# Hybrid retention and HGRN2 block on Trainium2: norm weights as 4 KB loads, spread over partitions by matmuls; four x loads on one landing

## The chip, the cores and the metric

The program runs on the 8 NeuronCores of one Trainium2 chip, the same code on each core with its own data: one prompt stream of 2048 frames and two running streams of 16 frames per core. Nothing is exchanged between cores. A time is device microseconds (us) of one execution, taken on the slowest core. The profile is one profiled execution; its page is that of the slowest core (core 7).

The engines are PE (matmuls), ACT, DVE and POOL (elementwise work) and SP, which here only issues DMAs. POOL also issues the DMAs that convert f32 to bf16 on the way, and those that add to their destination. Each engine runs its own list of instructions in order; semaphores order them between engines.

## The reference: what is computed

For x (frames x 1024), with RMSNorm over the 1024 channels before and after:

```
h = rmsnorm(x) * g_pre                      # g_pre: one vector of 1024
u = h @ W_in                                # 1024 x 4096, eight segments of 512 columns
rq, rk, rv, rg, hq, hf, hi, hg = split(u)
retention (4 heads of 128): rotary q, k; decayed state S_ret; o_r
HGRN2     (4 heads of 128): f = lb + (1 - lb) * sigmoid(hf); gated recurrence; o_h
o = concat(silu(rg) * headnorm(o_r), silu(hg) * headnorm(o_h))
y = x + rmsnorm(o @ W_out) * g_post         # g_post: one vector of 1024
```

The new states of both head groups are outputs too.

## The kernel before

**Tiling.** The prompt's 2048 frames are 4 blocks of 4 tiles of 128 frames. `front(k)` does for a block what needs all four tiles: `stage_A` per tile (load x, square sum on ACT at L670, the inverse root on POOL at L673 and L676, scaling by it and by `gpre` on DVE at L679, transposition into `xT` by PE at L693 with an ACT eviction at L697 for blocks 0 and 1, by DMA at L685 later), then `stage_B_hg` per HGRN2 head: the two projections of segments 5 and 4 (L714), the gate on ACT (L766, L768), forward and backward scans on DVE (`fG` L773, `fR` L785), and products on POOL (`KTh` L781, `QTh` L791). The scans work in two sets of buffers, so the projection of a third head waits for the first head's `fR` and `QTh`. `tile(k, j)` does the rest of a tile: the retention projections (segments 0 and 1, L731) with the rotary products (DVE L806, L810, POOL L819), V and gates (segments 2, 6, 3, 7, L731), `stage_D` (scores L895 into `AT`, outputs L927 and L932, new states L944 into `Sst` by DVE at L949 or L952, head norms) and `stage_E` (transposition of `og` into `ogT`, the output projection L1009, the norm with `gpost` at L1027, the residual). A block of two short sample streams follows with block 3; its states are loaded at L1096, `sret` and `shg`, into the `xs` and `xbf` buffers.

**Norm weights.** `g_pre` and `g_post` arrive from the host already repeated over 128 partitions, 512 KB each, and are loaded as they are (L618, L620). The load of gpost is held back until the last load of W_in has landed.

**Weights.** W_in is loaded by ten DMAs of POOL (L603) with conversion to bf16: four of 512 KB (as bf16) for columns 0 to 1023, then six of 1 MB for columns 1024 to 4095, then two of 1 MB for W_out. PE reads a segment once its loads have landed.

**x tiles.** They alternate between two buffers `xs`. Tiles 2 and 3 use the two `xr` buffers, which else hold outputs. The loads of tiles 4 and 5, the first of block 1, wait for the load of segments 4 and 5 of W_in (`('Wi', 5, 3)`), and tiles 6 and 7 for a free `xs` buffer.

**Order.** The program first lists all operations with their reads and writes, and `Sched.list_schedule` then writes the order of each engine by a model: costs per operation, a longest path as priority (plus a `boost` where one is set, plus random noise, `S.jitter`), eight PSUM banks that are given out, and a model of the two DMA queues (`Net`): 310 bytes/ns in all, 45% of it for the SP queue when both are in use, and 2 us of latency. That order is fixed in the program. Where the model sees PE idle, `add_fillers` puts small matmuls on the identity (L1128): as many as fit into each gap of the first 16 us, and groups of six later. Each operation still waits by semaphore for what it needs, so where the model's time for a landing is too early, the engine stands. One part of the model:

```
if e != POOL and o["nbytes"] < 120000 and len(net.queues[0]) > 1:
    o["lat"] += 3500.0
```

**The sample states.** The load of `shg` at L1096 lists the readers of its `xs` buffer as what it waits for, and the load of `sret` ahead of it is among these; so shg is issued when sret has landed, and all that follows in SP's list waits with it.

Of the kernel before, what the change touches and what calls it, by code (L numbers as in the profile page):

```python
# [9 lines left out]
ALU = mybir.AluOpType  # L10
AF = mybir.ActivationFunctionType
# [4 lines left out]
D_MODEL = 1024  # L16
# [61 lines left out]
class Sched:  # L78
    def __init__(self):
        self.ops = []  # L80
        self.last_w = {}
        self.readers = {}
        self.jitter = None

# [112 lines left out]
    def list_schedule(self):  # L197
        ops = self.ops
        n = len(ops)
# [50 lines left out]
        def landed(until):  # L250
            out = net.advance(until)
            for i, t in out:
                o = ops[i]
                t += o["lat"]
                o["t_land"] = t
                for sx in succ[i]:
                    ready_t[sx] = max(ready_t[sx], t + XLAT)
                    ndeps[sx] -= 1
                    if ndeps[sx] == 0:
                        avail[ops[sx]["eng"]].append(sx)  # L260
            return len(out)
# [230 lines left out]
def build_nc(limit=None, marks=None):  # L492
    nc = bass.Bass("TRN2", target_bir_lowering=False)

    def din(name, shape):
        return nc.dram_tensor(name, list(shape), F32, kind="ExternalInput").ap()
# [10 lines left out]
    g_pre = din("g_pre", [128, 1024])  # L507
    g_post = din("g_post", [128, 1024])
# [12 lines left out]
    with ExitStack() as st:  # L521
# [55 lines left out]
        def pb(v):  # L577
            return psum[v.idx]
# [39 lines left out]
        gid = S.op(SP, lambda e: e.dma_start(out=gpre[:], in_=g_pre), writes=["gpre"], dma_key="gpre")  # L618
        S.ops[gid]["boost"] = 19.5e6
        late_dma.append(S.op(SP, lambda e: e.dma_start(out=gpost[:], in_=g_post), writes=["gpost"], dma_key="gpost"))  # L620
# [27 lines left out]
        def stage_A(k, j):  # L648
# [5 lines left out]
            if i in (2, 3):  # L654
                xbuf, xkey = xr[slot], ("xr", slot)
# [4 lines left out]
            else:  # L660
                t0 = (k.b * 4 + j) * 128
                xid = S.op(SP, lambda e: e.dma_start(out=xbuf[:], in_=xp[t0:t0 + 128, :]), writes=[xkey], dma_key=xkey)
                if i < 4:
                    S.ops[xid]["boost"] = 20e6 - 1e6 * i
                elif i < 6:
                    S.ops[xid]["deps"].add(S.last_w[('Wi', 5, 3)])
# [14 lines left out]
                 reads=[xkey, ("rsx", sq), "gpre"], writes=[("xbf", slot)])  # L681
# [291 lines left out]
        def stage_E(k, j, vs):  # L973
# [28 lines left out]
            for n in range(2):  # L1002
# [13 lines left out]
                if not acc:  # L1016
# [3 lines left out]
                         reads=[y, "gpost"] + yd, writes=yk)  # L1020
# [4 lines left out]
            if acc:  # L1025
                for n in range(2):
# [3 lines left out]
                         reads=[ybk[n], "rs2", "gpost"], writes=[("xr", slot) if n == 0 else ("xr1", slot)])  # L1030
# [34 lines left out]
        def front(k):  # L1065
            for j in range(k.ns):
                stage_A(k, j)
            if k.b == 0:
                lb_chain()
# [59 lines left out]
        S.jitter = (13, 500.0)  # L1129
# [67 lines left out]
```

How the kernel before makes its waits and increments, by code:

```python
            def then_inc(self, *a, **k):  # L109
                return self
# [336 lines left out]
        def run(h, e):  # L447
            waited = {}
            for i in streams[e]:
                o = ops[i]
                req = {}
                for dpi in need[i]:
                    dp = ops[dpi]
                    key = id(dp["sem"])
                    if key not in req or req[key][1] < dp["val"]:
                        req[key] = (dp["sem"], dp["val"])
                for key, (sem, val) in req.items():
                    if waited.get(key, 0) >= val:
                        continue
                    h.wait_ge(sem, val)
                    waited[key] = val
                ins = o["fn"](h)
                if o["sig"]:
                    ins.then_inc(o["sem"], 16 if o["dma_key"] is not None else 1)
```

## Time and profile before

| | us |
|---|---|
| runs of the kernel before | 381.8, 383.2, 438.4 (median 383.2) |
| profiled execution, its own time | 382.7 |
| its span (core 7, first to last instruction) | 381.2 |
| spans of the other cores | 377.5 to 380.3 |

| engine | busy us | share of the span |
|---|---|---|
| PE | 357.4 | 94% |
| DVE | 237.9 | 62% |
| POOL | 218.7 | 57% |
| ACT | 183.9 | 48% |

Chain that ended last: PE 62%, DMA 21%, POOL 5%, issue 5%, ACT 3%, DVE 3%.

How to read it: the busy time of PE holds the fillers of the first 45 us, and matmuls overlap one another, so 94% is not 94% of useful work. A row of the chain says what was being waited for at that time. Of a DMA the profile gives the issue and the time from issue to landing. The landing of a load is the sum of both.

### The profile page before, as it was taken

What the parts mean: (1) busy time and instruction counts of PE and PEld (TensorE: products, weight loads), DVE (VectorE), ACT (ScalarE), POOL (GpSimd) and SP (SyncE); (2) the same over time, 40 slices, a digit from 0 to 9 for tenths busy, and PEclk for the clock granted to TensorE, in tenths of its full rate; (3) what the DMA queues carried; (4) which work ended last, traced back from release to release, by engine and by line L of the source; (5) the groups of instructions that cost most, each with busy time, mean ns of one, the idle gap of its engine ahead of it and who ended that gap; (6) DMA issues with size and microseconds to landing.
All of it is one profiled execution on the core that took longest, in us unless ns stands there. A gap on an engine that the chain in (4) does not pass through costs nothing.

```text
span 381.2 us, 8011 instructions; the slowest of 8 cores (377.5 to 381.2 us)
## 1 busy us (share of the span) xinstructions
PE 357.4 (94%) x2375; PEld 188.7 (50%) x2375; DVE 237.9 (62%) x524; ACT 183.9 (48%) x567; POOL 218.7 (57%) x292
## 2 busy tenths in 40 slices
PE   8989699689999999999979999999999999999993
PEld 8844354335455555444535454545454555545541
DVE  0137464684986975968656749486666464477545
ACT  2431242857878745463535252626353425435551
POOL 8425542557578776657446756575746365364630
PEclk9999899999999999999999999999999999999999
DMA  7999999997090997664566472525352556466714
GB/s 197 204 172 171 176 162 209 179 245 169 0 147 23 230 200 174 164 116 119 115 147 123 124 150 56 137 59 131 62 131 55 129 95 101 80 138 145 213 36 125
DMA packets 60619, 51.56 MB, mean 135 GB/s; under 512 B 41632, under 2 KB 48832, under 8 KB 60576
## 3 DMA queue, kind: packets, MB, share of 16 engines
q1 hardware_dynamic: 53104, 32.69, 34.4%
q0 software_dynamic: 7472, 18.35, 30.9%
q8 instruction: 20, 0.33, 0.4%
q14 instruction: 23, 0.19, 0.2%
HBM read 41.73 MB, written 10.09 MB: 136 GB/s over the span
## 4 chain that ended last, share of the span: by engine, by line
PE 62%; DMA 21%; POOL 5%; issue 5%; ACT 3%; DVE 3%; DVEq 0%; POOLq 0%; SPq 0%; ACTq 0%
PE bank L731 33%; PE bank L1009 14%; DMA Wi<-w_in 13%; PE bank L714 8%; DMA xs<-xp 5%; DMA xs<-sret 2%; PE bank L927 2%; PE bank L932 2%; PE bank L944 2%; PE bank L895 1%; POOL Wi L603 1%; DMA xT<-xbf 1%; DVE xbf L679 1%; POOL QTh L791 1%; POOL rsx L676 1%
## 5 line engine op out<-in xcount | busy, mean ns | idle before, releaser
L731 PE MATMUL bank<-Wi,xT 128*128 128x512 bf16 (+1 forms) x816 | 190.1, 381 | 1.7 <-ACT xT L697 0.7
L731 PEld LDWEIGHTS bank<-Wi,xT 128*128 128x128 bf16 (+1 forms) x816 | 77.5, 99 | 86.2 <-issue 6.0
L714 PE MATMUL bank<-xT,Wi 128*128 128x512 bf16 (+1 forms) x320 | 62.5, 342 | 4.8 <-POOL QTh L791 2.4
L965 DVE SCALAR_TENSOR_TENSOR og<-bank,rsq,gate 128x128 bf16<-128x128 f32 (+1 forms) x136 | 38.6, 343 | 43.9 <-POOL rsq L962 27.0
L1009 PE MATMUL bank<-Wo,ogT 128*128 128x512 bf16 (+1 forms) x272 | 62.8, 379 | 2.5 <-DVE Sst L949 2.5
L714 PEld LDWEIGHTS bank<-xT,Wi 128*128 128x128 bf16 x320 | 26.6, 98 | 36.5 <-issue 9.8
L1009 PEld LDWEIGHTS bank<-Wo,ogT 128*128 128x128 bf16 (+1 forms) x272 | 25.9, 98 | 31.2 <-issue 3.0
L884 POOL TENSOR_TENSOR Sst<-Sst,decS 128x512 f32<-128x512 f32 x30 | 31.4, 1049 | 16.4 <-DVE Sst L949 11.5
L955 ACT ACTIVATE og<-bank 128x128 bf16<-128x128 f32 (+1 forms) x136 | 35.5, 281 | 5.7 <-PE bank L927 3.7
L962 POOL TENSOR_TENSOR rsq<-ssq,mhalf 128x4 f32<-128x4 f32 (+1 forms) x34 | 34.7, 1021 | 4.4
L888 ACT ACTIVATE Sb<-Sst 128x512 bf16<-128x512 f32 x30 | 18.9, 630 | 36.7 <-POOL Sst L884 16.3
L854 ACT ACTIVATE gate<-bank 128x512 bf16<-128x512 f32 (+1 forms) x34 | 20.3, 598 | 30.0 <-PE bank L731 29.7
L781 POOL TENSOR_TENSOR KTh<-fG 128x512 bf16<-128x512 f32 (+1 forms) x20 | 18.8, 942 | 27.6 <-DVE fG L773 27.6
L773 DVE TENSOR_TENSOR_SCAN fG<-bank,zer 128x128 f32<-128x128 f32 (+1 forms) x72 | 23.3, 378 | 17.3 <-ACT bank L768 15.6
L679 DVE SCALAR_TENSOR_TENSOR xbf<-xs,rsx,gpre 128x1024 bf16<-128x1024 f32 (+1 forms) x15 | 22.5, 1511 | 17.7 <-POOL rsx L676 17.7
L819 POOL TENSOR_TENSOR qtm<-tA,tB 128x512 bf16<-128x512 f32 (+1 forms) x17 | 22.7, 1338 | 16.2 <-DVE tA L806 12.0
L1013 ACT ACTIVATE og<-bank 128x512 bf16<-128x512 f32 (+1 forms) x34 | 20.2, 595 | 22.8 <-PE bank L1009 22.8
L785 DVE TENSOR_TENSOR_SCAN fR<-bank,inv,zer 128x128 f32<-128x128 f32 (+1 forms) x72 | 28.0, 439 | 2.1 <-DVE inv L777 0.6
L955 ACT ACTIVATION_READ_ACCUMULATOR og<-bank 128x1 f32 (+1 forms) x136 | 29.0, 214 | 0.0
L791 POOL TENSOR_TENSOR QTh<-fQ,fR 128x512 bf16<-128x512 f32 (+1 forms) x20 | 22.8, 1140 | 8.8 <-ACT fQ L789 4.0
L819 POOL TENSOR_TENSOR Ktr<-tA,tB 128x512 bf16<-128x512 f32 (+1 forms) x17 | 22.5, 1322 | 8.5 <-DVE tA L806 6.2
L1027 DVE SCALAR_TENSOR_TENSOR xr<-bank,rs,gpost 128x512 f32<-128x512 f32 x30 | 21.5, 742 | 9.2 <-PE bank L714 4.8
(97 smaller groups left out, 457.9 us busy)
## 6 DMA issues: line engine op xcount, KB each, us to landing
xr<-xp POOLq DMA_DIRECT2D x15, 512.0 KB, 6.1
yp<-xr SPq DMA_DIRECT2D x15, 512.0 KB, 3.6
xs<-xp SPq DMA_DIRECT2D x14, 512.0 KB, 7.0
Wi<-w_in POOLq DMA_DIRECT2D x6, 1024.0 KB, 45.6
Wi<-w_in POOLq DMA_DIRECT2D x4, 512.0 KB, 19.0
Wo<-w_out POOLq DMA_DIRECT2D x2, 1024.0 KB, 73.8
xr<-xp SPq DMA_DIRECT2D x3, 512.0 KB, 11.2
rot<-rot_p SPq DMA_DIRECT2D x16, 96.0 KB, 6.3
```

Source lines behind the costliest of these rows:

```text
L679: S.op(DVE, lambda e: e.scalar_tensor_tensor(out=xbf[slot][0:L, :], in0=xbuf[0:L, :], scalar=rsx[0:L, sq:sq + 1], in1=gpre[0:L, :], op0=AL ...
L714: ins = e.matmul(pb(v)[:, 0:nt], lhsT=Wi[:, kc, col0:col0 + 128], rhs=k.xT[:, kc, 0:nt], start=(kc == 0), stop=(kc == 7))
L731: ins = e.matmul(pb(v)[0:L, :], lhsT=k.xT[:, kc, j * 128:j * 128 + L], rhs=Wi[:, kc, seg * 512:(seg + 1) * 512], start=(kc == 0), stop=(kc ...
L773: S.op(DVE, lambda e, c=c: e.tensor_tensor_scan(out=G[:, c, rsl(cl - 1, cl)], data0=pb(v)[:, rsl(c * st_ + cl - 1, cl)], data1=zer[:, 0:cl ...
L785: S.op(DVE, lambda e, c=c: e.tensor_tensor_scan(out=pack(R)[:, c, :], data0=pb(v)[:, c * st_:c * st_ + cl], data1=zer[:, 0:cl], initial=IV ...
L791: S.op(POOL, lambda e: e.tensor_tensor(out=tok(k.QT[:, h, :]), in0=pack(SQ), in1=pack(R), op=ALU.mult), reads=["fQ", ("fR", f)] + [("fR", ...
L819: S.op(POOL, lambda e, ts=ts, dst=dst: e.tensor_tensor(out=dst[0:L, :], in0=tA[ts][0:L, :], in1=tB[ts][0:L, :], op=ALU.add), reads=[("tA", ...
L884: S.op(POOL, lambda e, Sst=Sst, cc=cc, g=g, gsl=gsl: e.tensor_tensor(out=Sst[:, gsl].rearrange("p (h e) -> p h e", h=4), in0=Sst[:, gsl].r ...
L955: S.op(ACT, lambda e, q_=q_, h=h, vo=vo: e.activation(out=ogs[vs][0:L, h * 128:(h + 1) * 128], in_=pb(vo)[0:L, q_ * 128:(q_ + 1) * 128], f ...
L962: S.op(POOL, lambda e, gq=gq, g=g: e.tensor_tensor(out=rsq[vs][0:L, gq], in0=ssq[vs][0:L, gq], in1=mhalf[0:L, 0:4], op=ALU.pow), reads=[(" ...
L965: S.op(DVE, lambda e, q_=q_, h=h, vo=vo: e.scalar_tensor_tensor(out=ogs[vs][0:L, h * 128:(h + 1) * 128], in0=pb(vo)[0:L, q_ * 128:(q_ + 1) ...
L1009: ins = e.matmul(pb(y)[0:L, :], lhsT=ogT[:, kc, 0:L], rhs=Wo[:, kc, n * 512:(n + 1) * 512], start=(kc == 0), stop=(kc == 7))
```

## The change

- The host hands over `g_pre` and `g_post` as 8 x 128 values, 4 KB each. They are loaded into 8 partitions of `Sst`. ACT and DVE split the values into three bf16 parts whose sum is the f32 value (a part, and the rest twice), in `ogT`. A selector of 0 and 1 in `AT`, made from the identity by one DVE copy, spreads each row of 128 values over all partitions: 12 matmuls of 128 columns for each half of a vector, 48 in all, and one eviction for each half, on ACT for the first and on DVE for the second. All operations up to the end of g_pre's have the highest priority of all (`boost` 25e6), so the two small loads are first in SP's list. The f32 weights in `gpre` and `gpost` are as before, but nothing of the two 512 KB loads is left. Uses of AT, ogT and Sst come after.
- Tiles 6 and 7 go into `xr` like tiles 2 and 3, and their loads wait for the same landing as those of tiles 4 and 5. `stage_A` of block 1 is listed in block 0's `front`, ahead of block 0's gate work.
- The model takes each landing of a DMA issued by SP (transposes too) 2 us later than before (`slack`), and the noise is drawn anew (seed 10 for 13). Both, and the new operations, give each engine a new order.

```diff
@@ -254,7 +255,7 @@
                 t += o["lat"]
                 o["t_land"] = t
                 for sx in succ[i]:
-                    ready_t[sx] = max(ready_t[sx], t + XLAT)
+                    ready_t[sx] = max(ready_t[sx], t + XLAT + (self.slack if o["eng"] == SP or o["tr"] else 0.0))
                     ndeps[sx] -= 1
                     if ndeps[sx] == 0:
                         avail[ops[sx]["eng"]].append(sx)
...
@@ -504,8 +505,8 @@
     shg = din("shg", [2, 4, 128, 128])
     w_in = din("w_in", [1024, 4096])
     w_out = din("w_out", [1024, 1024])
-    g_pre = din("g_pre", [128, 1024])
-    g_post = din("g_post", [128, 1024])
+    g_pre = din("g_pre", [8, 128])
+    g_post = din("g_post", [8, 128])
     lbs = din("lbs", [128, 8])
     rot_p = din("rot_p", [SEQ, 192])
     rot_s = din("rot_s", [DEC_SEQ, 192])
...
@@ -615,9 +616,35 @@
         for i in range(NF):
             S.op(POOL, lambda e, i=i: e.memset(fG[i][:, :, CW - 1:CW], 1.0), writes=[("fG", i)])
 
-        gid = S.op(SP, lambda e: e.dma_start(out=gpre[:], in_=g_pre), writes=["gpre"], dma_key="gpre")
-        S.ops[gid]["boost"] = 19.5e6
-        late_dma.append(S.op(SP, lambda e: e.dma_start(out=gpost[:], in_=g_post), writes=["gpost"], dma_key="gpost"))
+        sel, g8, res, part = AT[0:8, :, :], Sst_p[0:8, 0:256], Sst_p[0:8, 256:512], ogT
+        n0 = len(S.ops)
+        for v, src in enumerate((g_pre, g_post)):
+            S.op(SP, lambda e, v=v, src=src: e.dma_start(out=g8[:, v * 128:(v + 1) * 128], in_=src), writes=[("g8", v)], dma_key=("g8", v))
+        S.op(DVE, lambda e: e.tensor_copy(out=sel, in_=ident[0:8, 0:8].unsqueeze(2).to_broadcast([8, 8, 128])),
+             reads=["ident"], writes=[("AT", 0), ("AT", 1)])
+        G8 = [("g8", 0), ("g8", 1)]
+        p2 = [part[0:8, 2 * i:2 * i + 2, :].rearrange("p a b -> p (a b)") for i in range(3)]
+        S.op(ACT, lambda e: e.activation(out=p2[0], in_=g8, func=AF.Copy), reads=G8, writes=["ogT"])
+        S.op(DVE, lambda e: e.tensor_tensor(out=res, in0=g8, in1=p2[0], op=ALU.subtract), reads=G8 + ["ogT"], writes=["S0"])
+        S.op(ACT, lambda e: e.activation(out=p2[1], in_=res, func=AF.Copy), reads=["S0"], writes=["ogT"])
+        S.op(DVE, lambda e: e.tensor_tensor(out=p2[2], in0=res, in1=p2[1], op=ALU.subtract), reads=["S0", "ogT"], writes=["ogT"])
+        for v, dst, key in ((0, gpre, "gpre"), (1, gpost, "gpost")):
+            for n in range(2):
+                T = S.bank()
+
+                def bc(e, v=v, n=n, T=T):
+                    ins = None
+                    for q in range(4):
+                        for i in range(3):
+                            ins = e.matmul(pb(T)[:, q * 128:(q + 1) * 128], lhsT=sel[:, n * 4 + q, :], rhs=part[0:8, 2 * i + v, :],
+                                           start=(i == 0), stop=(i == 2))
+                    return ins
+                S.op(PE, bc, reads=["ogT", ("AT", 0), ("AT", 1)], writes=[T])
+                S.op(ACT if n == 0 else DVE, (lambda e, dst=dst, T=T: e.activation(out=dst[:, 0:512], in_=pb(T)[:, :], func=AF.Copy)) if n == 0 else
+                     (lambda e, dst=dst, T=T: e.tensor_copy(out=dst[:, 512:1024], in_=pb(T)[:, :])), reads=[T, "S0"], writes=[(key, n)])
+            if v == 0:
+                for i, o in enumerate(S.ops[n0:]):
+                    o["boost"] = 25e6 - 1e4 * i
         S.op(SP, lambda e: e.dma_start(out=tkT[:], in_=tk), writes=["tk"], dma_key="tk")
         S.op(SP, lambda e: e.dma_start(out=glT[:], in_=gl), writes=["glT"], dma_key="glT")
         S.op(SP, lambda e: e.dma_start(out=lbt[:], in_=lbs.rearrange("p (r h) -> p r h", r=2)), writes=["lbt"], dma_key="lbt")
...
@@ -651,7 +678,7 @@
             slot = i % 2
             L = k.rows
             xbuf, xkey = xs[slot], ("xs", slot)
-            if i in (2, 3):
+            if i in (2, 3, 6, 7):
                 xbuf, xkey = xr[slot], ("xr", slot)
             if k.sample:
                 S.op(POOL, lambda e: e.memset(xbuf[0:LS, :], 0.0), writes=[xkey])
...
@@ -662,7 +689,7 @@
                 xid = S.op(SP, lambda e: e.dma_start(out=xbuf[:], in_=xp[t0:t0 + 128, :]), writes=[xkey], dma_key=xkey)
                 if i < 4:
                     S.ops[xid]["boost"] = 20e6 - 1e6 * i
-                elif i < 6:
+                elif i < 8:
                     S.ops[xid]["deps"].add(S.last_w[('Wi', 5, 3)])
             n0 = len(S.ops)
             junk, jk = (xbf[slot], [("xbf", slot)]) if i >= 4 else (gate[i], [("gate", i, 0), ("gate", i, 512)])
...
@@ -1063,9 +1090,12 @@
             return rid
 
         def front(k):
-            for j in range(k.ns):
-                stage_A(k, j)
+            if k.b != 1:
+                for j in range(k.ns):
+                    stage_A(k, j)
             if k.b == 0:
+                for j in range(4):
+                    stage_A(blocks[1], j)
                 lb_chain()
             if k.sample or k.b < 2:
                 set_ret_dec(k)
...
@@ -1126,7 +1156,8 @@
 
         def filler_fn(e, k):
             return e.matmul(psum[k][:, 0:128], lhsT=ident[:], rhs=ident[:], start=True, stop=True)
-        S.jitter = (13, 500.0)
+        S.slack = 2000.0
+        S.jitter = (10, 500.0)
         S.emit(nc, st, filler=(filler_fn, ident_ready, 700.0, 400.0, 60.0, 16000.0, 1300.0, 6))
     return nc
 
...
@@ -1180,8 +1211,8 @@
         m["shg"] = np.ascontiguousarray(state_hgrn[0, 2 * c:2 * c + 2])
         m["w_in"] = w_in[0]
         m["w_out"] = w_out[0]
-        m["g_pre"] = np.ascontiguousarray(np.broadcast_to(g_pre, (128, D_MODEL)))
-        m["g_post"] = np.ascontiguousarray(np.broadcast_to(g_post.reshape(1, D_MODEL), (128, D_MODEL)))
+        m["g_pre"] = np.ascontiguousarray(g_pre.reshape(8, 128))
+        m["g_post"] = np.ascontiguousarray(g_post.reshape(8, 128))
         m["lbs"] = np.ascontiguousarray(lower_bounds.reshape(2, 4, 128).transpose(2, 0, 1)).reshape(128, 8)
         in_maps.append(m)
     res = run_bass_kernel_spmd(nc, in_maps, core_ids=list(range(N_CORES)))
```

The uses of `gpre` at L679 now wait for both of its halves, those of `gpost` at L1018 and L1027 for the half that they read.

## Rows read from the trace of the kernel before

**Rows 1.** Cores view: span from first to last instruction and mean granted clock.

```profile
core 1: 380.3 us, clock 0.986
core 2: 378.6 us, clock 0.987
...
core 7: 381.2 us, clock 0.991
```

**Rows 2.** Core 7 stages: length; busy PE, PEld, DVE, ACT, POOL; clock; DMA; GB/s.

```profile
66.00:100.00 34.00, 27.78 (x171) 13.75 (x171) 22.97 (x50) 24.32 (x48) 19.84 (x24) 1.00 0.82 172
...
190.00:200.00 10.00, 7.48 (x47) 3.75 (x46) 5.97 (x12) 3.14 (x7) 4.54 (x6) 1.00 0.66 159
200.00:350.00 150.00, 149.90 (x927) 76.26 (x926) 94.62 (x213) 67.08 (x244) 87.81 (x112) 1.00 0.52 107
...
70.00:80.00 10.00, 6.72 (x42) 3.13 (x40) 9.41 (x24) 6.86 (x12) 5.01 (x5) 1.00 1.06 191
```

**Rows 3.** Chain that ended last, core 7, first 125 us: start, length.

```profile
8.37 48.39 DMA Wi<-w_in
56.93 9.86 DMA xs<-xp
...
71.55 8.62 DMA xs<-xp
```

**Rows 4.** Loads of Wi: all ten, fifth and sixth; a PE wait.

```profile
L603 POOL DMA_DIRECT2D Wi<-w_in x10: 741/781/965, 2.0 to 9.9; - x10
...
DMA to landing us min/median/max: 14.1/33.6/62.2
...
L603 POOL DMA_DIRECT2D Wi<-w_in x2: 792/796/800, 5.1 to 5.8; - x2
DMA to landing us min/median/max: 30.7/33.6/36.6
...
28.87 4.91 PE L731 MATMUL bank<-Wi,xT 128*128 128x512 bf16 x22 [0.63 <-DMA Wi<-w_in]
```

**Rows 5.** From issue to landing: the load of gpre, the xs loads.

```profile
gpre<-g_pre SPq DMA_DIRECT2D x1, 512.0 KB, 5.7
...
DMA to landing us min/median/max: 3.9/7.0/12.3
```

**Rows 6.** What PE waited for, 56 to 100 us, core 7: total, times, longest.

```profile
PE bank L714 <- POOL QTh L791: 2.4, 2, 1.5
PE bank L714 <- DVE fR L785: 2.1, 1, 2.1
```

**Rows 7.** The x scaling of L679 (ns min/median/max), and a meeting with POOL.

```profile
L679 DVE SCALAR_TENSOR_TENSOR xbf<-xs,rsx,gpre x14: 1257/1285/2240, 8.7 to 177.4; 128x1024 bf16<-128x1024 f32 x14
...
82.60 2.21 DVE L679 SCALAR_TENSOR_TENSOR xbf<-xs,rsx,gpre 128x1024 bf16<-128x1024 f32 x1 [1.18 <-POOL rsx L676]
...
82.46 1.26 POOL L791 TENSOR_TENSOR QTh<-fQ,fR 128x512 bf16<-128x512 f32 x1
```

**Rows 8.** SP at the sample states, cores 7, 0; then PE wait.

```profile
179.81 0.39 SPq L1096 DMA_DIRECT2D xs<-sret  x1
188.08 0.37 SPq L1096 DMA_DIRECT2D xs<-shg  x1
...
179.06 0.38 SPq L1096 DMA_DIRECT2D xs<-sret  x1
184.33 0.37 SPq L1096 DMA_DIRECT2D xs<-shg  x1
...
PE bank L1009 <- DVE Sst L949: 2.5, 1, 2.5
```

**Rows 9.** Core 7, first 45 us: fillers, first x tile.

```profile
L1128 PE MATMUL bank<-ident 128*128 128x128 bf16 x235 | 16.8, 239 | 3.3 <-POOL ident L591 1.9 <-DVE tB L810 1.2 <-POOL rsx L676 0.2
...
8.67 1.28 DVE L679 SCALAR_TENSOR_TENSOR xbf<-xs,rsx,gpre 128x1024 bf16<-128x1024 f32 x1 [7.47 <-POOL rsx L676]
...
11.00 0.61 PE L693 MATMUL bank<-ident,xbf 128*128 128x128 bf16 x8
```

More of the change, by code:

```diff
@@ L83, in __init__ @@
         self.jitter = None
+        self.slack = 0.0
     def op(self, eng, fn, reads=(), writes=(), dma_key=None, deps=()):
@@ L680, in stage_A @@
                                                        in1=gpre[0:L, :], op0=ALU.mult, op1=ALU.mult),
-                 reads=[xkey, ("rsx", sq), "gpre"], writes=[("xbf", slot)])
+                 reads=[xkey, ("rsx", sq), ("gpre", 0), ("gpre", 1)], writes=[("xbf", slot)])
             if i == 3:
@@ L1019, in stage_E @@
                                                                   in1=gpost[0:L, n * 512:(n + 1) * 512], op=ALU.mult),
-                         reads=[y, "gpost"] + yd, writes=yk)
+                         reads=[y, ("gpost", n)] + yd, writes=yk)
             S.op(POOL, lambda e: e.tensor_scalar(out=rs2[0:L, :], in0=ss2[0:L, 0:1], scalar1=ss2[0:L, 1:2], scalar2=EPS,
@@ L1029, in stage_E @@
                                                                     op0=ALU.mult, op1=ALU.mult),
-                         reads=[ybk[n], "rs2", "gpost"], writes=[("xr", slot) if n == 0 else ("xr1", slot)])
+                         reads=[ybk[n], "rs2", ("gpost", n)], writes=[("xr", slot) if n == 0 else ("xr1", slot)])
                 S.op(POOL, lambda e: e.dma_start(out=xr[slot][:], in_=xp[t0:t0 + 128, :], accum_op=ALU.add),
```

## The prediction

> **What bounds the kernel now.** I read the view of the cores first. The profiled execution took 382.7 us, 1.5 us more than the span of core 7, the slowest; the median of the runs shown is 383.2 and the other undisturbed one 381.8, so the profiled one stands for them. Cores 1 and 7 are some 2 us behind core 2 [rows 1], so something happens on those two alone, and the time is theirs.
>
> Then the stages of core 7. From 66 to 100 us PE is busy 27.8 of 34 us, so 6.2 us are idle; from 190 to 200 us it is busy 7.5 of 10 [rows 2]. From 200 to 350 us it is full (149.9 of 150). So the kernel is a DMA-bound front, a PE-bound body with one hole, and a tail; only what shortens the front, the hole or the tail can pay.
>
> The chain that ended last shows the front: from 8.4 to 56.8 us it is a load of Wi, then x loads of 9.9 and 8.6 us [rows 3]. The ten Wi loads land from 2.0+14.1 = 16.1 to 9.9+62.2 = 72.1 us; the fifth (5.1+30.7 = 35.8) and the one at 56.8 stand three loads of 1 MB (as bf16) apart, so 7.0 us each [rows 3, 4]. PE does wait for them: at 28.9 us its queue is released by a Wi landing [rows 4]. The x loads of block 1 hang on the landing at 56.8, and the third and fourth are issued only once an xs buffer is free, the third at 71.5 us [rows 3].
>
> Third, the hole at 195 us. On core 7 the load of sret is issued at 179.8 and shg, behind it in SP's queue, at 188.1: 8.3 us. On core 0 the same step takes 5.3 us. Core 7's PE then waits 2.5 us [rows 8]. The x of that time, its transpose and the sample norm are queued on SP behind this pair. So a planned order met a landing later than planned, on the slowest cores only.
>
> **The change part by part.** *g_pre as 4 KB.* One 512 KB load leaves the start; it took 5.7 us to land [rows 5]. What does it cost the Wi stream? Lower bound: the last two Wi loads took 72.1 - 56.8 = 15.3 us with two x loads beside them, against 14.0 for two alone [rows 3, 4]; 0.65 us per x load. Upper bound: gpre took 5.7 us to land, x tile 0 just ahead of it 3.9 [rows 5]; with 0.4 us between two issues (the length of one, rows 8) that is 2.2 us of the queue's time. I take 1.5, in the middle, since at the start five such loads stand beside the stream. The stream moves up by that and PE's front with it: **-1.5 us** (-2.2 to -0.6).
>
> *Building gpre from parts.* Two small loads go first in SP's queue; the x tiles behind them are issued about 2 x 0.4 us later, 0.4 us being the length of one issue [rows 8]. Then come a selector copy, two casts on ACT, two subtractions on DVE, 24 matmuls for gpre with one eviction each on ACT and DVE, and the same 24 and two for gpost. Now the first x tile is scaled at 8.7 us and transposed at 11.0, but the first Wi lands only at 16.1 [rows 4, 9]. Even if gpre is ready at 13 us, 4 us late, it costs nothing: the cover is the first Wi load, and the fillers, 235 of them with 16.8 us busy [rows 9], shrink or grow with it. If the cover were gone, each us late would be one us lost. The 24 matmuls of gpost use AT, ogT and Sst as scratch, so they must be done before the first scores and may fall where PE has real work. Eight 128-column matmuls take 0.61 us [rows 9], so 24 take at most 1.8 us, at least 0 in the place of fillers. I take a third: **+0.6 us**.
>
> *g_post as 4 KB.* Its 512 KB now wait for the last Wi load (72.1 us) and run beside Wo and the last x tiles of block 1; nothing needs them before block 0's first output, and PE waits for no Wo or gpost up to 100 us. 0, at most the 0.65 to 2.2 us of the load above, kept in the range.
>
> *Four early x loads.* All four tiles of block 1 are issued at the Wi landing, tiles 6 and 7 into xr, which is idle until block 0's first output. The first two x loads took 9.9 and 12.3 us [rows 3, 5], so they landed 2.8 us apart (12.3 - 9.9 + 0.4 between issues); the planner itself counts 512 KB at 45% of 310 bytes/ns, 3.8 us. At 3.3 us between, four land at about 10, 13, 16.5 and 20 us after the first issue, the last at 55.4+20 = 75, where now already the third lands only at 71.5+8.6 = 80.2 [rows 3]. By bytes 0.65 us per load moves from after the Wi stream into it; the last Wi load comes later by up to 1.3 us less the 1.5 gained. What PE gains is at most the 6.2 idle us of 66 to 100. But its waits there are named: 2.4 us for POOL's QTh and 2.1 for DVE's fR [rows 6], so three quarters stand behind the forget-gate chain of block 0, not behind x. More tiles give the planner other work to put there, yet DVE is busy 9.4 of 10 us from 70 to 80 [rows 2], and two more scalings of at least 1.3 us want in. Bounds: all of the 4.5 us gone, or the two scalings paid in full at their longest, 2 x 2.2 = 4.4 us [rows 7]. I take **-2.0 us**, a third of the idle time: nearer to the gain, since PE's own order is what leaves it empty.
>
> *Later landings, and another draw of the jitter.* The planner's order is written anew for all engines, with every SP landing taken 2 us later. Its model gives sret 2.0 us plus 256 KB at 45% of 310 bytes/ns, 3.9 us in all; measured 8.3 and 5.3 [rows 8]. With 2 us more it plans for 5.9: core 0 is then covered, core 7 short by 2.4 in place of 4.4, and a 2.5 us wait becomes about 0.4. Also the first x of block 1 (9.9 us against a modelled 5.8) is met better. When the hole closes the slowest core falls back to core 2's kind, 2.6 us less [rows 1]. I take **-2.3 us** (-2.6 to 0). Elsewhere a new order opens or closes single waits; the ones seen now are 2.1 to 2.5 us, so 0 with 2.5 either way. The slack also stretches the planned life of each tile; the four slots for tiles in flight cover that.
>
> Sum: 382.7 - 1.5 + 0.6 - 2.0 - 2.3 = **377.5 us**, 1.5% under the median.
>
> **A rule beside the trace.** In the trace a scaling begun at 82.60 while POOL's multiply of 82.46 ran took 2.2 us, against a median of 1.3 [rows 7]; it ended about 1 us late, as if it had stood until POOL was done. The Trainium skill (SBUF — State Buffer, Who interferes with whom) says that a DVE instruction with two SBUF inputs and a GpSimd instruction that reads SBUF exclude each other, and the later one waits. That speaks against the change: two more such scalings move into the stretch in which POOL makes KTh and QTh. By the rule the third rival below gets its upper price, without it the lower.
>
> **The rivals.** *All of it pays.* The stream gains 2.2 and no wait of 66 to 100 stays (-4.5), the hole closes fully (-2.6): 382.7 - 2.2 - 4.5 - 2.6 = 373.4. For it: these are all waits in one in-order queue, and late landings explain several. Against: the named waits are for DVE and POOL, which have as much to do as before.
>
> *The transfer was hidden anyway.* The chain of the forget gate sets 66 to 100 us as before and the hole stays, since core 7's sret is still later than planned: 382.7 - 1.5 + 0.6 = 381.8. For it: rows 6 and the 2.4 us that are still short. Against: four tiles instead of two to choose from.
>
> *Slower: the scalings block the gate chain.* If all four x scalings come ahead of the third head's scans, each blocked to 2.2 us where now two of 1.3 stand, DVE is late by 4 x 2.2 - 2 x 1.3 = 6.2 us, and PE with it, since those scans free the buffers of the next projections: 382.7 + 6.2 - 1.5 - 2.3 = 385.1. It outweighs the gains from a delay of 3.8 us. For it: DVE is 94% busy just there. Against: the planner weighs DVE's time and gives these scalings no boost.
>
> *The change does not do what it says.* The scheme for gpre takes so long that x is late: after 16.1 us each us costs one. It would need 5 us more than now; with 6 us, 378.5, inside the range.
>
> **How the numbers follow.** Forecast 0.50 (its own range 374 to 381), all pays 0.20, hidden anyway 0.16, slower 0.12, late gpre 0.02. The range leaves a tenth on either side: 372.3 to 385.5. A measurement of this kernel can tell about 2% from no change, that is 375.5 and 390.9. Faster: all of the first rival and a quarter of the forecast, 0.33. Slower by over 2% needs the blocked scalings and two new waits: 0.05. Same: 0.62.
>
> **What would show it.** Right: no 512 KB load of g; the Wi landing now at 56.8 at about 55.3; four x issues together there, the fourth landing near 75; PE idle 66 to 100 down from 6.2 to about 4; no wait for DVE Sst near 195; cores 1 and 7 level with the rest; gpre's evictions before 9 us. Wrong: a first x transpose later than 16 us; scalings of 2.2 us ahead of scans with PE waiting for fR; new waits of PE behind transposes after 100 us; a tail that ends over 2 us later after PE's last full stage.

## The result and the profile after

| | before | changed |
|---|---|---|
| median of the runs | 382.95 us | 378.62 us |
| lowest, highest | 381.78, 438.44 | 378.21, 378.79 |
| profiled execution, its own time | 382.71 | 378.74 |
| its span | 381.2 (core 7) | 377.1 (core 2) |

The ratio is 0.9889 with a 95% interval of 0.9868 to 0.9911: 1.1% faster, 4.3 us. Forecast were 377.5 us and a range of 372.3 to 385.5. Executions in which one die's cores ran at a lower clock than the other's are left out of every comparison, and in e1 and e3, where cores 0 to 3 stayed behind in the rest too, cores 4 to 7 are read.

The view of the cores of the changed kernel, against [rows 1]:

```profile
core 1: 376.6 us, clock 0.989
core 2: 377.1 us, clock 0.985
...
core 7: 377.0 us, clock 0.985
```

The gain has two parts. The middle one of the eight core spans fell from 378.3 us to 376.9 in the profiled executions, and the slowest core now lies 0.2 us above it, where core 7 lay 2.9 us above it. In the control run below (4 executions against 21 of the kernel before) the middle core gains 3.0 us, and the distance from it to the slowest falls from 2.4 to 1.1.

The stages of core 2, columns as in [rows 2] (length; busy PE, PEld, DVE, ACT, POOL; clock; DMA; GB/s):

```profile
66.00:100.00 34.00, 32.81 (x208) 17.01 (x207) 25.54 (x59) 26.32 (x55) 18.90 (x26) 1.00 0.67 143
...
190.00:200.00 10.00, 10.00 (x65) 5.14 (x64) 8.92 (x16) 3.47 (x7) 5.30 (x5) 1.00 0.69 103
200.00:350.00 150.00, 147.67 (x928) 75.05 (x926) 90.62 (x207) 66.54 (x248) 88.31 (x115) 1.00 0.50 107
```

The idle time of PE from 66 to 100 us fell from 6.2 us on core 7 to 1.2, and the hole near 195 is gone. But from 200 to 350 us PE, busy for 149.9 us before, is now busy for 147.7.

What PE waited for, 56 to 100 us, then 100 to 365 us (total, times, longest), against [rows 6]:

```profile
PE bank L720 <- DVE xbf L706: 0.6, 1, 0.6
PE bank L758 <- DVE fR L812: 0.6, 1, 0.6
...
PE bank L758 <- ACT fQ L816: 1.3, 1, 1.3
PE bank L922 <- DVE Sst L976: 0.5, 1, 0.5
```

The waits for QTh are gone, that for fR is down from 2.1 to 0.6, and two of 0.6 us are what is left. Behind 100 us small ones have come, the longest 1.3 us.

The four x loads. SP's issues (start, length), then the fourth load's time to landing:

```profile
56.53 1.05 SPq L689 DMA_DIRECT2D xs<-xp  x2
57.73 1.26 SPq L689 DMA_DIRECT2D xr<-xp  x2
...
L689 SPq DMA_DIRECT2D xr<-xp x1: 622/622/622, 58.4 to 58.4; - x1
...
DMA to landing us min/median/max: 17.9/17.9/17.9
```

All are issued within 2.3 us; the fourth lands at 58.4+17.9 = 76.3. The others took 9.8, 12.1 and 15.2 us, so the four landed at 9.8, 12.6, 16.4 and 19.8 us after the first issue.

Three of the four loads of segments 2 to 5 of W_in (issues from 5.8 to 7.3 us), against [rows 4]:

```profile
L604 POOL DMA_DIRECT2D Wi<-w_in x3: 792/800/808, 5.8 to 7.3; - x3
DMA to landing us min/median/max: 35.0/42.6/49.2
```

The last of them lands at 7.3+49.2 = 56.5 us, where it was 56.8. The tenth and last Wi load lands later than before: at 75.4 us in place of 72.5, mean of the eight cores. No core's PE waits for it.

The start: PE's timeline, then the first cast on ACT and the last subtraction on DVE, against [rows 9]:

```profile
1.86 8.10 PE L1158 MATMUL bank<-ident 128*128 128x128 bf16 x95 [1.86 <-POOL mhalf L594]
9.89 2.85 PE L639 MATMUL bank<-ogT,AT 8*128 8x128 bf16 x48
...
15.14 0.61 PE L720 MATMUL bank<-ident,xbf 128*128 128x128 bf16 x8 [0.46 <-DVE xbf L706]
...
18.18 1.02 PE L758 MATMUL bank<-Wi,xT 128*128 128x512 bf16 x4
...
3.13 0.41 ACT L627 ACTIVATE ogT<-Sst 8x256 bf16<-8x256 f32 x1 [0.35 <-DMA Sst<-g_post]
...
4.67 0.41 DVE L630 TENSOR_TENSOR ogT<-Sst,ogT 8x256 bf16<-8x256 f32 x1 [0.61 <-ACT ogT L629]
```

The parts of the weights are ready at 4.67+0.41 = 5.1 us, but PE has 95 fillers ahead of the 48 spreading matmuls, 8.1 us long, and begins them at 9.9. The transposes of the first x tile come at 15.1 in place of 11.0 us, and the first projection at 18.2 in place of 17.0, though the first load of W_in now lands at 14.2. The evictions of gpre come at 10.8 and 11.5 us.

### The profile page after: what moved, and what is told of

The parts are those of the page before. It is cut to its first block, busy times and chain, and to the rows that moved or that the text cites. A ratio compares the mean times of both kernels' runs of the same rounds, so it can differ in the third digit from the quotient of the medians.

```text
span 377.1 us, 8007 instructions; the slowest of 8 cores (375.1 to 377.1 us)
## 1 busy us (share of the span) xinstructions
PE 357.0 (95%) x2371; PEld 188.7 (50%) x2371; DVE 238.9 (63%) x529; ACT 185.9 (49%) x571; POOL 217.8 (58%) x292
## 4 chain that ended last, share of the span: by engine, by line
PE 82%; DVE 5%; issue 4%; POOL 4%; ACT 4%; DVEq 0%; POOLq 0%; ACTq 0%
PE bank L758 43%; PE bank L1036 15%; PE bank L741 13%; PE bank L1158 2%; PE bank L954 2%; PE bank L959 2%; PE bank L971 2%; PE bank L922 2%; ACT og L982 1%; DVE xbf L706 1%; POOL rsx L703 1%; PE bank L720 1%; POOL qtm L846 1%; ACT gate L697 1%; DVE Sst L976 1%
## 5 line engine op out<-in xcount | busy, mean ns | idle before, releaser
L1036 PEld LDWEIGHTS bank<-Wo,ogT 128*128 128x128 bf16 (+1 forms) x272 | 25.9, 98 | 29.3 <-issue 1.0
L976 DVE TENSOR_TENSOR Sst<-bank,Sst 128x512 f32<-128x512 f32 x30 | 20.3, 687 | 24.3 <-PE bank L971 24.0
L846 POOL TENSOR_TENSOR qtm<-tA,tB 128x512 bf16<-128x512 f32 (+1 forms) x17 | 21.9, 1288 | 19.9 <-DVE tB L837 16.8
L808 POOL TENSOR_TENSOR KTh<-fG 128x512 bf16<-128x512 f32 (+1 forms) x20 | 18.0, 910 | 23.1 <-DVE fG L800 19.6
L982 ACT ACTIVATION_READ_ACCUMULATOR og<-bank 128x1 f32 (+1 forms) x136 | 29.8, 219 | 0.0
L930 DVE TENSOR_TENSOR AT<-bank,maskT 128x512 bf16<-128x512 f32 x32 | 21.2, 685 | 11.6 <-PE bank L922 11.5
L833 DVE TENSOR_TENSOR tA<-bank,rot 128x512 f32<-128x512 f32 (+1 forms) x34 | 23.0, 681 | 7.0 <-PE bank L758 4.4
```

Of the source, the lines that this page charges most:

```text
L846: S.op(POOL, lambda e, ts=ts, dst=dst: e.tensor_tensor(out=dst[0:L, :], in0=tA[ts][0:L, :], in1=tB[ts][0:L, :], op=ALU.add), reads=[("tA", ...
L976: S.op(DVE, lambda e, vd=vd, Sst=Sst, gsl=gsl: e.tensor_tensor(out=Sst[:, gsl], in0=pb(vd)[:, :], in1=Sst[:, gsl], op=ALU.add), reads=[vd, ...
L982: S.op(ACT, lambda e, q_=q_, h=h, vo=vo: e.activation(out=ogs[vs][0:L, h * 128:(h + 1) * 128], in_=pb(vo)[0:L, q_ * 128:(q_ + 1) * 128], f ...
L1036: ins = e.matmul(pb(y)[0:L, :], lhsT=ogT[:, kc, 0:L], rhs=Wo[:, kc, n * 512:(n + 1) * 512], start=(kc == 0), stop=(kc == 7))
```

## The experiments

All but the control are edits of one of the two kernels. Some keep the order of every engine and change only a wait or a load, the others have their order planned anew. For all of them there is one measure beside the ratio: the middle core, the mean over runs of the median of the eight core spans.

The runs come from three chips, e1 to e4 from one, e5 to e8 from a second, e9 to e12 from a third, each with the kernel before beside them. The changed kernel without an edit ran on the second alone, and the chip of the first measurement is not on record. On the first chip cores 0 to 3 are 2 to 3 us behind cores 4 to 7 in e1, e2 and e3, the edits of the changed kernel, and 0.3 us in the kernel before. Whether the changed kernel itself loses its gain there was not run. On cores 4 to 7 the kernel before takes 378.7 us on the first and the second chip, so these cores can be compared across the two.

| run | edit of | median us | ratio to before (95%) | middle core, before beside it |
|---|---|---|---|---|
| e1_dummy448 | changed, order kept | 385.4 | 1.005 (1.002 to 1.008) | 379.0, 378.9 |
| e2_x67_late | changed, order kept | 391.0 | 1.020 (1.016 to 1.024) | 387.0, 378.9 |
| e3_40_fillers | changed, order kept | 385.0 | 1.002 (0.998 to 1.006) | 377.4, 378.9 |
| e4_shg_free | before, order kept | 382.7 | 1.000 (0.997 to 1.002) | 378.8, 378.9 |
| e5_after_again | changed, control | 378.5 | 0.989 (0.983 to 0.995) | 375.7, 378.7 |
| e6_x_only | before | 386.7 | 1.009 (1.005 to 1.013) | 383.3, 378.7 |
| e7_g_only | before | 383.5 | 1.002 (0.997 to 1.006) | 379.9, 378.7 |
| e8_slack_only | before | 383.7 | 1.004 (1.001 to 1.007) | 380.7, 378.7 |
| e9_seed13 | changed | 381.0 | 0.998 (0.996 to 1.000) | 377.9, 378.4 |
| e10_seed11 | changed | 384.8 | 1.010 (1.006 to 1.014) | 381.6, 378.4 |
| e11_no_slack | changed | 385.4 | 1.014 (1.009 to 1.018) | 381.9, 378.4 |
| e12_g_512 | changed | 382.1 | 1.000 (0.998 to 1.003) | 378.7, 378.4 |

The second table says where the time is. It is worked out from the stage view of all eight cores of each profiled execution: the length of a stage less PE's busy time in it, median of the cores. In each trace two of the cores lack some 40 matmul records, which reads there as 1 to 2 us more of idle time; the median is little moved by them. The last stage runs from 365 us to each core's end. "Low clock" is the mean over the cores of (1 - granted clock) x length, summed to 365 us.

| idle us of PE | 28-60 | 60-100 | 100-200 | 200-365 | 365-end | low clock |
|---|---|---|---|---|---|---|
| before | 3.7 | 4.7 | 0.8 | 0.2 | 7.0 | 3.5 |
| changed | 3.8 | 1.3 | 1.0 | 2.5 | 6.5 | 3.2 |
| changed, control | 3.6 | 1.3 | 1.0 | 2.6 | 6.5 | 2.8 |
| e2 x 6, 7 late | 3.8 | 7.5 | 1.6 | 2.6 | 6.7 | 9.0 |
| e6 x only | 4.3 | 3.8 | 4.6 | 0.3 | 7.0 | 3.6 |
| e7 g only | 3.1 | 6.0 | 0.8 | 1.8 | 7.0 | 3.8 |
| e8 slack only | 2.6 | 3.8 | 3.8 | 1.5 | 6.7 | 3.7 |
| e9 seed 13 | 2.7 | 2.0 | 1.1 | 2.8 | 6.9 | 2.7 |
| e10 seed 11 | 3.0 | 3.1 | 1.4 | 3.1 | 8.6 | 1.6 |
| e11 no slack | 3.3 | 2.6 | 3.8 | 1.5 | 7.6 | 6.1 |
| e12 g 512 KB | 3.1 | 2.4 | 3.9 | 0.8 | 6.8 | 3.6 |

Idle time before 28 us is left out, since fillers cover it.

**A load of 448 KB put back (e1).**

```diff
+        dumT = sb("dumT", [128, 896], F32)
+        S.extra = lambda e: e.dma_start(out=dumT[:], in_=xp[0:128, 0:896])
+            k_ = [ops[i]["dma_key"] for i in order[SP]].index(("xs", 0)) + 1
+            order[SP].insert(k_, len(ops))
```

> The changed kernel, every engine's order kept, with one 448 KB load of x rows into an unused tensor put back behind the first x load; its data is not used. Theory A (what the prediction said: one such load holds the Wi stream up by 0.65 to 2.2 us and PE's front with it): the Wi landing at 56 us comes about 1.3 us later and the time is 1 to 1.5 us over the changed kernel's 378.6. Rival B (the stream has its own pace and swallows the load before the Wi landings that PE waits for): first Wi landing about 1 us later, the one at 56 us within 0.5 us, time within 0.5 us of 378.6.

The Wi landing of 56 us came at 57.7 to 59.9 us on the eight cores (mean 58.8), against 55.0 to 57.0 (56.1) in the control. What PE waited for, core 3:

```profile
PE bank L749 <- DMA Wi<-w_in: 1.8, 1, 1.8
```

On core 3 that wait is not there in the changed kernel. Over all cores it is 0.4 to 1.8 us on five of them here, 0.4 us on one in the changed kernel and 1.0 us on two in the control. On cores 4 to 7 the middle span was 378.3, 2.4 us over the control's 375.9 (on cores 0 to 3 it was 381.2). So Theory A in kind and more than it in size: in a fixed order a load of that size in the first microseconds costs 2.7 us of stream and 2.4 us of time.

Taking such a load away, in orders that were planned anew, gives less. Landings of Wi loads in us, mean over the eight cores of each trace:

| Wi load | 1st | 4th | 6th | 8th (range over kernels) |
|---|---|---|---|---|
| g_pre as 512 KB (before, e4, e6, e8, e12) | 16.7 | 28.9 | 42.8 | 56.9 (56.6 to 57.5) |
| g_pre as 4 KB (changed, e2, e3, e5, e7, e9, e10, e11) | 15.6 | 27.9 | 41.9 | 56.1 (55.6 to 56.5) |
| e1, 4 KB and the extra load | 15.4 | 29.3 | 43.8 | 58.8 |

The first two groups do not overlap in any column: without the 512 KB load the landing of 56 us comes 0.8 us sooner. Why the extra load of e1 costs three times that is open. Its rows of 3584 bytes in place of 4096 are one difference; this was not tried.

**x tiles 6 and 7 late (e2).**

```diff
+            if i in (4, 5):
+                norm45.append(len(S.ops) - 1)
+            if i in (6, 7):
+                S.late.append((xid, norm45[i - 6]))
+        for a_, b_ in self.late:
+            ops[a_]["deps"].add(b_)
```

> The changed kernel, order kept, but the loads of x tiles 6 and 7 wait until tiles 4 and 5 are scaled, as in the kernel before. Theory A (the early loads are what emptied the idle time of 66 to 100 us): tiles 6 and 7 land some 8 us later, PE idles 3 to 6 us more between 66 and 100 us, time 381 to 384. Rival B (it is the new order of the gate chain, not the landings): PE idles under 1 us more, time under 379.5.

SP's issues on core 1 (start, length), and PE's wait (total, times, longest):

```profile
56.28 1.11 SPq L693 DMA_DIRECT2D xs<-xp  x2
75.44 0.92 SPq L693 DMA_DIRECT2D xr<-xp  x2
...
PE bank L728 <- DVE xbf L710: 6.7, 1, 6.7
```

Tiles 6 and 7 are issued at 75.4 us, 17.7 us later than in the changed kernel, and PE waits 6.7 us for the scaling. They land at 84.5 and 87.8 us, 12 us later than in the changed kernel where 8 were expected, and 4 us later than in the kernel before, so the stall is larger than one that the change took away. Idle time of 60 to 100 us rose from 1.3 to 7.5 us, and the low clock from 2.8 to 9.0. Theory A: in this order the early landings are what PE lives on. The time, 391.0, is over the 384 expected, which held neither the clock nor so late a landing; on cores 4 to 7 the middle span is 385.9, 10 us over the control's.

**40 fillers (e3).**

```diff
+                first = next(k_ for k_, i in enumerate(order[PE]) if ops[i]["line"] != 0)
+                order[PE] = order[PE][:40] + order[PE][first:]
```

> The changed kernel, order kept, with 40 in place of 95 filler matmuls ahead of the 48 matmuls that spread the weights. Theory A (those fillers, planned at 60 ns and taking 85, kept the spreading until 9.9 us though its parts were there at 5.1, and this made the first x tile and PE's first projection 1.2 us late): the spreading starts at 5 to 6 us, the first projection at 15 to 16.5 in place of 18.2, time 1 to 2 us under 378.6. Rival B (PE is held by Wi landings and by the retention chain until 57 us anyway): first projection earlier, but the stage from 42 us on starts as before and the time is within 0.5 us of 378.6. Rival C: fewer matmuls early and a lower granted clock, slower.

PE's timeline on core 6, then its first stage:

```profile
1.85 4.13 PE L1160 MATMUL bank<-ident 128*128 128x128 bf16 x40 [1.85 <-POOL mhalf L596]
5.91 2.85 PE L641 MATMUL bank<-ogT,AT 8*128 8x128 bf16 x48
...
16.65 1.03 PE L760 MATMUL bank<-Wi,xT 128*128 128x512 bf16 x4
...
0.00:28.00 28.00, 22.02 (x227) 17.02 (x228) 9.04 (x21) 11.85 (x19) 16.52 (x34) 0.94 0.93 175
```

The spreading starts at 5.9 us, 4 us sooner, and the first projection at 16.7 on this core; by the median of the eight cores it is 17.0 against 18.1 in the control, 1.1 us sooner. The first gate projection, which needs the Wi landing of 56 us, starts at 56.5 us on the middle one of cores 4 to 7 (57.1 in the control), and the middle span of these cores is 375.9, the control's to 0.1 us. So Rival B: the late first x tile costs nothing, being swallowed before 57 us. The granted clock of the first stage is 0.94 in the mean of the eight cores, against 0.97 in the changed kernel and 0.96 in the control, which hints at C, but cores 4 to 7 show no loss. The ratio is that of cores 0 to 3 and is not used for the edit.

**shg without sret (e4).**

```diff
+            if o["dma_key"] is not None and o["dma_key"][0] == "sld":
+                o["deps"] = {d for d in o["deps"] if not (ops[d]["dma_key"] is not None and ops[d]["dma_key"][0] == "sld")}
```

> The kernel before, order kept, but the load of shg no longer waits for that of sret (they write different halves of the buffer). Theory A (the 8.3 us that SP stood there on core 7 is what made cores 1 and 7 late by 2.5 us): the two loads issue 0.5 us apart, no PE wait for DVE Sst near 195 us, cores 1 and 7 level with the others, time 380 to 380.7 in place of 382.8. Rival B (the sret landing itself, or another late DMA, holds the sample chain): the wait stays and the time is within 0.7 us of 382.8.

SP's issues on core 7 (start, length), then PE's longest wait after 100 us there:

```profile
180.37 0.39 SPq L1098 DMA_DIRECT2D xs<-sret  x1
180.81 0.74 SPq L1098 DMA_DIRECT2D xs<-shg  x1
...
PE bank L946 <- ACT Kth L922: 0.5, 1, 0.5
```

The two loads are 0.4 us apart, no wait for DVE Sst of 2.5 us is left on any core, and the time is what it was, 0.9996. Neither theory: the wait did vanish, and with it went nothing. In 23 executions of the kernel before beside this run, cores 1 and 7 are no slower than the others (middle spans 379.0 and 378.6 in 378.5 to 379.4), and each of the eight cores is the slowest in some of them. So the hole of [rows 8] is not what these executions lose their time by. How often it comes is not shown: other executions of the kernel before left no trace, and in the one of e4 sret landed 5.6 to 6.5 us after its issue, where cores 1 and 7 of the kernel before, the two with the hole, have 7.5 and 8.2 us and the six without it 5.2 to 6.2.

**The control (e5).**

> The changed kernel once more, unchanged, as the control beside the next three and for the earlier edits of it. Theory A (its gain holds wherever it runs): ratio to the kernel before 0.985 to 0.993, some 379 us. Rival B (part of the 4.3 us is the spread between cores in one execution, which on this chip is larger): ratio 0.994 to 1.0, with the middle cores still 2 to 3 us ahead of the kernel before.

Theory A in the ratio, 0.9886, as in the first measurement. Of the 4.4 us of the ratio 3.0 are the middle core's; the rest is the distance of the slowest core from it, 1.1 us in place of 2.4. So Rival B is right in that a part lies there.

**Each part alone (e6, e7, e8).**

```diff
# e6: as in the change
+            if i in (2, 3, 6, 7):
+                elif i < 8:
+                    stage_A(blocks[1], j)
# e7: the change with these taken back
-        S.slack = 2000.0
-        S.jitter = (10, 500.0)
# e8
+        S.slack = 2000.0
```

> The kernel before with one part of the change: four early x loads, stage A of block 1 listed ahead; the 512 KB loads of g, the landings as planned before and seed 13 stay. Theory A (the early loads carry the gain): PE idle 66 to 100 us falls from 6.2 to 1 to 3 us, middle cores 2 to 4 us ahead of the kernel before. Rival B (without the later landings the planner asks for tiles 6 and 7 too soon): PE waits 2 us or more for a scaled x tile, time within 1 us of before or above it.

> The kernel before with one part of the change: both norm weights as 4 KB loads spread by matmuls; x loads, landings and seed as before. Theory A (the transfer is worth 1 us or less, and the spreading makes the first x tile late only when landings are planned 2 us later): fillers ahead of the spreading fewer than 95, first projection at 16 to 17.5 us, middle cores 0 to 1.5 us ahead of before. Rival B (a full 512 KB off the early queue is worth more): 2 us or more ahead, with the Wi landing at 56 us over 1.5 us earlier.

> The kernel before with one part of the change: the planner takes SP's landings 2 us later; loads and seed as before. Theory A (the slack alone only redraws the order; what it removes are rare waits on late landings, which cost little): middle cores within 1.5 us of before. Rival B (the slack carries a third or more of the gain, by fewer waits behind x loads and transposes): 1.5 to 3 us ahead, PE's waits for scaled x tiles gone.

None is faster than the kernel before; by the middle core they are 4.6, 1.2 and 2.0 us slower. Early x alone (what PE waited for, 40 to 382 us, core 6):

```profile
PE bank L714 <- DVE fR L785: 3.3, 1, 3.3
PE bank L927 <- DVE AT L903: 1.8, 1, 1.8
PE bank L731 <- DVE Sst L949: 1.5, 3, 0.7
```

There the idle time of 60 to 100 us falls only from 4.7 to 3.8, behind the gate scans of DVE and not behind x, and 3.8 us come up between 100 and 200. With 4 KB weights alone (PE's timeline, core 4):

```profile
1.85 5.90 PE L1155 MATMUL bank<-ident 128*128 128x128 bf16 x62 [1.85 <-POOL mhalf L594]
7.69 3.15 PE L639 MATMUL bank<-ogT,AT 8*128 8x128 bf16 x48
...
16.47 2.12 PE L758 MATMUL bank<-Wi,xT 128*128 128x512 bf16 x8
```

The spreading has 62 fillers ahead, not 95, and the first projection starts at 16.5: the slack is what adds fillers (e11, without it and with seed 10, has 62 too). The first gate projection starts at 56.3 us, 2.2 us sooner than before, yet 60 to 100 us idles 6.0 us. The slack alone has 3.0 us more of idle time from 100 to 200, though each operation keeps its noise of before (same seed, same list). So Rival B of e6 only in its number, Theory A of e7 in its start but not its gain, and neither of e8: each part alone does something of what it should in its own place and pays for it elsewhere.

**The draw (e9, e10).**

```diff
-        S.jitter = (10, 500.0)
+        S.jitter = (13, 500.0)      # e9;  (11, 500.0) in e10
```

> All parts of the change but the new draw: seed 13 in place of 10. Theory A (4 KB weights, early loads and later landings work only together, whatever the draw): middle cores 2 to 3 us ahead of the kernel before, ratio 0.985 to 0.993. Rival B (the draw of the order carries the gain; a draw moves the time by some 3 us either way): ratio 0.996 to 1.01, with PE idle in other stages than in the changed kernel.

> The changed kernel with seed 11 in place of 10, a third draw of the same program. Theory A (the parts together carry it): ratio 0.985 to 0.993 like seed 10. Rival B (the draw carries it): 0.996 to 1.01, and a different stage than with seed 13 holds the loss.

What PE waited for from 100 to 365 us in e9, core 4, and in e10, core 3:

```profile
PE bank L954 <- DVE fR L812: 1.5, 1, 1.5
PE bank L1036 <- ACT ogT L1026: 0.7, 1, 0.7
```

```profile
PE bank L758 <- DVE Sst L976: 1.5, 4, 0.5
PE bank L954 <- DVE fG L800: 1.0, 1, 1.0
```

The same program in three draws runs at 0.989, 0.998 and 1.010 of the kernel before. All three have less idle time from 60 to 100 us than before (1.3, 2.0 and 3.1 against 4.7) and more after it; seed 11 has 2.1 us more in the tail as well. Rival B: in two of three draws the changed program is at most 0.2% faster than the kernel before. Other draws of the kernel before were not run, so what the change is worth over draws is open.

**Without the later landings, and with the 512 KB weights (e11, e12).**

```diff
-        S.slack = 2000.0
+        S.slack = 0.0               # e11
# e12: the kernel before with
+        S.slack = 2000.0
+        S.jitter = (10, 500.0)
+            if i in (2, 3, 6, 7):
...
```

> All parts of the change but the later landings (slack 0, seed 10). Theory A (the early loads need the later landings, since the planner else asks for tiles 6 and 7 too soon): idle time of 60 to 100 us back to 3 to 5 us, waits for scaled x tiles or the gate scans, ratio over 0.996. Rival B (the draw of seed 10): ratio stays under 0.993.

> All parts of the change but the 4 KB weights: early loads, later landings, seed 10, and both 512 KB loads as before. Theory A (the dummy load put back at fixed order cost 6 us in time by holding up the Wi landing of 56 us by 2 us or more; the 4 KB weights are worth that much): ratio 0.998 to 1.005, PE waiting for Wi between 42 and 60 us. Rival B (an order planned with the 512 KB load in it bears it): ratio 0.985 to 0.995.

In e11 the time of Theory A comes by another way: the idle time of 60 to 100 us is 2.6 us, not back at 4.7, and the loss is at 100 to 200, with a lower clock. What PE waited for there, core 3:

```profile
PE bank L1036 <- DVE fR L812: 1.4, 1, 1.4
PE bank L922 <- DVE Sst L976: 1.3, 1, 1.3
```

These are DVE's gate scans and states, no landings. e12 has Theory A's ratio, 1.000, and only a part of its cause: PE waits 0.8 to 1.5 us for Wi between 30 and 66 us, and 3.9 us of idle time lie in 100 to 200. Taking an operation into the list or out of it draws the noise anew for all that follow, and e11, which keeps the noise, still has another order. By the middle core e12 (378.7) lies inside the spread of e9 and e10, and e11 (381.9) at its edge (381.6), so neither tells a part's worth.

## Why the prediction was right, point by point

**The time and the range.** 378.6 against 377.5; the sum was short by 1.1 us. The single terms were less good than their sum: one stage gave more than its term, the body took it back, and that the two nearly cancel is luck, as is the draw, since the same program with two other seeds ran at 0.998 and 1.010 of the kernel before.

**g_pre as 4 KB, -1.5 us.** The first Wi load lands 0.9 us sooner in the mean of the eight cores (15.7 against 16.6 us; 15.4 in the control), the one of 56 us 0.4 us sooner (56.2 against 56.6; 56.1 in the control). Over all kernels with and without the 512 KB load it is 1.1 us at the first and 0.8 at 56 us, inside the bounds of 0.6 and 2.2; in a fixed order (e1) such a load weighs 2.4 to 2.7 us, over the upper bound. The first gate projection starts at 58.1 and, in the control, 57.1 us, against 58.5 (medians of the cores), so PE's front moved by 0.4 to 1.4 us in place of 1.5.

**Building gpre, hidden.** Hidden in effect, but "its cover is the first Wi load" failed: the first projection comes 1.2 us later, since the fillers ahead of the spreading neither shrank nor moved. The sign "evictions before 9 us" failed with it. The planner counts 60 ns for one filler, 95 of them took 8.1 us (85 ns each), and with landings planned 2 us later it put more ahead. e3 shows that the real cover is deeper: it is the Wi landing of 56 us. The 48 matmuls took 2.9 us among fillers, so the +0.6 us for gpost fell away.

**Four early x loads, -2.0 us.** Landings at 9.8, 12.6, 16.4 and 19.8 us after the issue, against 10, 13, 16.5 and 20. Idle time of 60 to 100 us fell by 3.4 us in the median core and the low clock there by 1.0, more than the term. e2 shows that it hangs on the landings; e6, that it takes an order which uses them. The price of the loads was too low: "0.65 us per load" came from two loads beside the last two of Wi, and two more made these 3 to 4 us longer (last section).

**Later landings, -2.3 us for the hole.** This step failed. "Something happens on those two alone, and the time is theirs" was read from one execution. e4 takes the cause away and nothing follows in ten executions. What stands in its place is the slowest core's distance from the middle one: 2.5, 2.4 and 1.8 us in the three sets of runs of the kernel before, 0.8 and 1.1 in the two of the changed one. It gives 1.3 us or so. That this comes of the slack is not shown: slack alone (e8) has 1.2, x alone 1.9 and g alone 2.4 on one chip; on another the changed kernel without slack (e11) has 2.9, but e9, e10 and e12, with slack, have 1.5, 1.8 and 1.6, where the kernel before has 1.8.

**The rest, 0 with 2.5 either way.** The second step that failed. The kernel before idles 0.6 us from 100 to 365 us on the four cores with all records and no hole (1.0 by the table); every one of the eight other orders planned idles 2.6 to 5.3 there. So its order was a good draw in the body, and all eight new ones lost there: 2.5 to 2.9 us here. This ate what 60 to 100 us gave above its term.

**The sum as it came out**, middle core, from the tables: 60 to 100 us -3.4 and clock there -1.0, front -0.4 to -1.4, body +2.5 to +2.9, tail -0.5: -2.4 to -3.8. Over the executions of the control run the middle core gained 3.0. But in the profiled executions, of which these rows are, it fell by 1.4 us only, and by 2.2 to the control's, so the sum does not close: 1.0 to 1.6 us of loss are in none of its terms. 0.4 us of it is more low clock after 365 us; the rest is open. The distance between the cores adds -1.3 to -1.7.

**The rivals.** *All of it pays* had its stage right and its end wrong, the body being the reason. *Hidden anyway* has its number, 381.8, near e9 (381.0), but the idle time fell there too. *Slower: the scalings block the gate chain*: in the changed kernel the scalings of tiles 4 and 5 took 1.3 us each. Those of 6 and 7, on DVE, beside POOL's product:

```profile
80.32 3.49 DVE L706 SCALAR_TENSOR_TENSOR xbf<-xr,rsx,gpre 128x1024 bf16<-128x1024 f32 x2 [1.18 <-POOL ssx L700]
...
81.32 1.42 POOL L818 TENSOR_TENSOR QTh<-fQ,fR 128x512 bf16<-128x512 f32 x1 [0.43 <-ACT fQ L816]
```

The second of the pair began at 81.5 us and took 2.3 us, beside POOL's QTh of 81.32, and ended 1.1 us after it. The Trainium skill (SBUF — State Buffer, Who interferes with whom) says that a DVE instruction with two SBUF inputs contends with a GpSimd instruction that reads SBUF; the trace agrees, as the scaling took 1.0 us longer than the first of the pair. But the planner put the pair behind the scans of the fourth head, and PE needed the second tile late. PE's transposes of the two tiles:

```profile
81.75 0.61 PE L720 MATMUL bank<-ident,xbf 128*128 128x128 bf16 x8 [0.62 <-DVE xbf L706]
...
85.87 0.61 PE L720 MATMUL bank<-ident,xbf 128*128 128x128 bf16 x8
```

The wait of 0.6 us is behind the first scaling, which was not blocked; the transposes that need the blocked one start 2.1 us after its end, without a wait. The price per scaling was right, and the place wrong: it cost PE nothing.

## What to carry to other kernels

When a program plans its own order, an edit is two edits: what it says, and a new draw of everything else. Here three draws of one program spread over 2%, more than any part alone moved the time, so a part's worth shows only with the order held still (e1 to e4), or over several draws. A wait in one profiled execution on the slowest core is no loss of the kernel until other executions show the same core late at the same place.

## What was not expected of the hardware

The Wi stream keeps most of what it gains by a load taken from its first microseconds: 1.1 us at the landing of 16 us, 0.8 us at that of 56 (the table of e1). Loads beside its end cost it more than their bytes: from the eighth to the tenth Wi landing it is 15.9 to 16.4 us with two x loads beside them (before, e2, e4, e7, e8) and 19.1 to 21.2 with four (the nine others), so some 1.9 us for each further load, where the prediction took 0.65.

And in e2 a stall came with a lower clock: 6.2 us more of idle time between 60 and 100 us and 6.2 us more of low clock over the run, 4.8 of them between 60 and 100 us. There the granted clock is 0.86 to 0.91 on the eight cores, where it is 1.00 on all of the control. The middle core was 11 us later than in the control, 10 us on cores 4 to 7.
